# Three chunks of modulation weights move from the second attention into the FFN before it, with a ring of four piece buffers and three accumulators

## What is computed

```python
c_act = jax.nn.silu(c)
for layer in range(DEPTH_2):
    mod = (c_act @ ada_w[layer] + ada_b[layer]).reshape(B, 3, 3, D_MODEL)
    h = modulate(x, norm_g[layer, 0], mod[:, 0, 0], mod[:, 0, 1])
    x = x + 0.5 * mod[:, 0, 2][:, None, :] * swiglu(h, ffn_w13[layer, 0], ffn_w2[layer, 0])
    h = modulate(x, norm_g[layer, 1], mod[:, 1, 0], mod[:, 1, 1])
    y = swa_mixer(...) if layer % N_MIXERS == 0 else fox_mixer(...)
    x = x + mod[:, 1, 2][:, None, :] * y
    h = modulate(x, norm_g[layer, 2], mod[:, 2, 0], mod[:, 2, 1])
    x = x + 0.5 * mod[:, 2, 2][:, None, :] * swiglu(h, ffn_w13[layer, 1], ffn_w2[layer, 1])
```

## Time and profile before

| | |
|---|---|
| median of 3 runs | 1521.77 us (1520.66 to 1526.52) |
| profiled execution | 1525.41 us |
| its span, first to last instruction | 1523.60 us |
| mean granted TensorE clock | 0.969 |
| PE busy | 1424.1 us (93%) |
| DVE busy | 1083.2 us (71%) |
| ACT busy | 732.8 us (48%) |
| POOL busy | 140.3 us (9%) |
| moved by DMA | 333.89 MB, mean 219 GB/s |

### The profile page before, as it was taken

The page is one execution under the profiler, slowest core; times in us unless marked ns, Lnnn a source line. Parts: engine busy times, 40 slices in busy tenths (PEclk is TensorE's granted clock), DMA queues, the critical chain, the costliest instruction groups (busy, mean ns, idle before and its releaser), DMA issues.

```text
span 1523.6 us, 18395 instructions
## 1 busy us (share of the span) xinstructions
PE 1424.1 (93%) x7241; PEld 1170.0 (77%) x7241; DVE 1083.2 (71%) x1523; ACT 732.8 (48%) x1036; POOL 140.3 (9%) x198
## 2 busy tenths in 40 slices
PE   2799898999999999988899999999999899999998
PEld 1588887999978877765688777787877766688886
DVE  5867885988977777767578777777777445566544
ACT  3454355444564433766463334644437566554432
POOL 1100100110101111000001111011120100000000
PEclk9899999999999999995999999999999989999999
DMA  9776664877859888461478887598883631376552
GB/s 355 237 226 204 229 213 143 270 254 246 307 180 311 291 280 290 140 221 28 141 244 300 295 284 256 179 309 296 282 282 115 197 110 56 111 243 199 177 184 81
DMA packets 189289, 333.89 MB, mean 219 GB/s; under 512 B 8834, under 2 KB 132462, under 8 KB 188180
## 3 DMA queue, kind: packets, MB, share of 16 engines
q1 hardware_dynamic: 161392, 236.02, 45.8%
q0 software_dynamic: 27232, 96.47, 19.3%
q10 hardware_dynamic: 580, 0.23, 0.1%
HBM read 331.53 MB, written 1.15 MB: 218 GB/s over the span
## 4 chain that ended last, share of the span: by engine, by line
PE 66%; DVE 15%; DMA 8%; ACT 6%; issue 4%; SPq 0%; ACTq 0%; POOL 0%; DVEq 0%; POOLq 0%
DMA ada<-in_ada_w 8%; PE bank L1449 8%; PE bank L1451 8%; PE bank L1450 8%; PE bank L1412 7%; PE bank L1414 6%; PE bank L1413 6%; DVE lo L942 5%; DVE ada_sum L901 4%; PE bank L1344 3%; PE bank L1345 3%; PE bank L1346 3%; ACT hi L514 2%; PE bank L1577 2%; PE bank L1650 2%
## 5 line engine op out<-in xcount | busy, mean ns | idle before, releaser
L942 DVE TENSOR_TENSOR lo<-raw,hi 128x2048 fp32r<-128x2048 f32 x215 | 490.9, 2286 | 67.3 <-ACT hi L514 66.8
L514 ACT ACTIVATE hi<-raw 128x2048 fp32r<-128x2048 f32 x215 | 405.6, 1909 | 34.6 <-DMA raw<-in_w_out 20.8
L1449 PE MATMUL bank<-hi,h_hi 128*128 128x512 f32 x704 | 277.9, 395 | 2.4 <-DVE lo L942 1.6
L901 DVE SCALAR_TENSOR_TENSOR ada_sum<-ada,c_act,ada_sum 128x512 f32<-128x512 f32 x308 | 231.1, 750 | 67.0 <-DMA ada<-in_ada_w 59.2
L1451 PE MATMUL bank<-hi,h_lo 128*128 128x512 f32 x704 | 274.5, 390 | 0.0
L1450 PE MATMUL bank<-lo,h_hi 128*128 128x512 f32 x704 | 274.1, 389 | 0.0
L470 POOL DMA_DIRECT2D ada<-in_ada_w x176 | 125.6, 714 | 1126.9 <-DVE ada_sum L901 1087.6
L1412 PE MATMUL bank<-hi,o_hi 128*128 128x512 f32 x504 | 206.1, 409 | 12.2 <-DVE lo L942 11.1
L1414 PE MATMUL bank<-hi,o_lo 128*128 128x512 f32 x504 | 198.3, 393 | 0.0
L1413 PE MATMUL bank<-lo,o_hi 128*128 128x512 f32 x504 | 197.8, 392 | 0.0
L625 ACT ACTIVATE KT<-bank 128x256 f32<-128x256 f32 x88 | 33.8, 384 | 315.9 <-PE bank L1451 315.8
(11 more groups left out here) (208 smaller groups left out, 1838.2 us busy)
## 6 DMA issues: line engine op xcount, KB each, us to landing
ada<-in_ada_w POOLq DMA_DIRECT2D x176, 512.0 KB, 5.3
raw<-in_ffn_w SPq DMA_DIRECT2D x176, 512.0 KB, 5.1
raw<-in_ffn_w SPq DMA_DIRECT2D x44, 1024.0 KB, 6.1
raw<-in_w_up SPq DMA_DIRECT2D x22, 1024.0 KB, 5.5
raw<-in_w_in SPq DMA_DIRECT2D x16, 1024.0 KB, 8.3
raw<-in_fox_w_in SPq DMA_DIRECT2D x12, 1024.0 KB, 5.1
raw<-in_w_down SPq DMA_DIRECT2D x11, 1024.0 KB, 6.2
raw<-in_swa_w_in SPq DMA_DIRECT2D x6, 1024.0 KB, 5.1
```

Source lines behind the costliest of these rows:

```text
L514: nc.scalar.activation(hi[:, n % NS, :], raw[:, n % NS, :], ACT.Copy).then_inc(hi_ready, 1)
L901: nc.vector.scalar_tensor_tensor(acc, in0=src, scalar=c_act[:, col:col + 1], in1=acc, op0=ALU.mult, op1=ALU.add).then_inc(ada_step, 1)
L942: nc.vector.tensor_tensor(lo[:, n % NS, :], raw[:, n % NS, :], hi[:, n % NS, :].bitcast(F32), ALU.subtract).then_inc(lo_ready, 1)
L1449: mm(bank[:, :], xk_hi, wh[:, i, :], start=k == 0, stop=False, skip_group_check=True)
```

## The change

The FFN before the second attention takes in twelve chunks in place of nine, and the attention none in place of three. Since twelve chunks are 48 pieces over 26 units, from unit 2 on (before: 36 over 27, from unit 3 on), the tables of that stage are drawn up anew: two pieces on most of the units 2 to 26, one on the units 8, 14, 21 and 27. From the second stage on the pieces go round four buffers: two of `ada` and two in `V`, which POOL may fill once the attention before has read its last values (and the first attention's pooling branch is done); in turn ACT waits with an attention's first value copy until all pieces of the stages before are used (L669). The accumulators `ada_sum` are three. In the first attention three turned sums, their column sums and a gate stand one unit later. At the entrance of the conv stage ACT and DVE take the second half of the rows before unit 3 and not behind it. The constants that were one tile (`kon`) are three tiles with two loads; two unused parts of them are no longer loaded. (`ident` becomes `ident[:, :]` in PE's calls, `c % 2` becomes `c % 3` where accumulators are read, `n % 2` becomes `slot`; these lines are not shown.)

```diff
-CHUNKS_IN = [6, 6, 9, 3, 9, 9, 0, 2]
+CHUNKS_IN = [6, 6, 12, 0, 9, 9, 0, 2]
+RING_FROM = PIECES * CHUNKS_IN[0]
...
     if kind0 in ("conv", "ffn"):
-        at = [3 + (p0 * 27 // (4 * n0) if n0 > 4 else p0) for p0 in range(4 * n0)]
...
+        from0, over = (2, 26) if n0 > 10 else (3, 27)
         turns, at_sums = [], []
-        for u1 in (at[4 * c0 + 3] + 2 for c0 in range(n0)):
+        for c0 in range(n0):
+            for p0 in range(4 * c0, 4 * c0 + 4):
+                u0 = from0 + (p0 * over // (4 * n0) if n0 > 4 else p0)
+                if c0 > 2:
+                    u0 = max(u0, at_sums[c0 - 3])
+                PIECES_AT[w0 + u0] = PIECES_AT.get(w0 + u0, 0) + 1
+            u1 = u0 + 2
...
-        SUMS_AT.update({w0 + u: 1 for u in (7, 9, 13, 16, 18, 21)})
-        COLS_AT.update({w0 + u: 1 for u in (8, 10, 14, 17, 19, 22)})
-        GATES_AT[w0 + 15], GATES_AT[w0 + 20] = (s0, 0), (s0, 1)
-    elif kind0 == "swa":
-        PIECES_AT[w0 + 4] = 2
-PIECES_STEP = {"moba": (), "swa": range(8, 16), "fox": ()}
-SUMS_STEP = {"moba": (), "swa": (1,), "fox": ()}
-COLS_STEP = {"moba": (), "swa": (2,), "fox": ()}
-SUMS_LAST = {"swa": 2, "fox": 0}
+        SUMS_AT.update({w0 + u: 1 for u in (7, 9, 13, 17, 19, 22)})
+        COLS_AT.update({w0 + u: 1 for u in (8, 10, 14, 18, 20, 23)})
+        GATES_AT[w0 + 15], GATES_AT[w0 + 21] = (s0, 0), (s0, 1)
...
-        ada_sum = sb("ada_sum", [P, 2, 512])
+        ada_sum = sb("ada_sum", [P, 3, 512])
...
+        def piece_slot(n):
+            if n < RING_FROM:
+                return n % 2, n // 2 + 1
+            q = n % 4
+            return q, (n - RING_FROM) // 4 + 1 + (RING_FROM // 2 if q < 2 else 0)
+
+        def piece_of(n):
+            q, _ = piece_slot(n)
+            return ada[:, q, :, :] if q < 2 else V[:, q - 2, :].rearrange("p (a b) -> p a b", a=2)
...
-                    if n > 1:
-                        pool.wait_ge(ada_step, 2 * (n - 1))
+                    slot, _ = piece_slot(n)
+                    if n < 2:
+                        pool.wait_ge(pro_step, KD)
                     else:
-                        pool.wait_ge(pro_step, KD)
-                    pool.dma_start(ada[:, n % 2, :, :], ...).then_inc(ada_full[n % 2], 16)
+                        earlier = n - 2 if n < RING_FROM + 4 else n - 4
+                        pool.wait_ge(ada_step, 2 * (earlier + 1))
+                    if slot >= 2:
+                        before = sum(n >= PIECES * sum(CHUNKS_IN[:s + 1]) for s in ATTENTIONS)
+                        pool.wait_ge(pv_done, (8, 24, 40)[before - 1])
+                        if before == 1:
+                            pool.wait_ge(pool_ready, 4)
+                    pool.dma_start(piece_of(n), ...).then_inc(ada_full[slot], 16)
...
                 if KINDS[b] == "conv":
                     normed(b, 1)
+                    modulated(b, 1)
                     split_to(W0[b] + 3)
...
+                if s and v == 0:
+                    act.wait_ge(ada_step, 2 * PIECES * sum(CHUNKS_IN[:s]))
...
                     if c >= PRO_CHUNKS + 3:
                         dve.wait_ge(ada_used, c - 2 - PRO_CHUNKS)
...
                     root(b, 1)
                     split_to(W0[b] + 2)
+                    split_h(b, 1)
+                    split_to(W0[b] + 3)
                 else:
                     split_to(W0[b] + 2)
                     root(b, 1)
-                split_to(W0[b] + 3)
-                split_h(b, 1)
+                    split_to(W0[b] + 3)
+                    split_h(b, 1)
...
-                columns(int(t in COLS_STEP[kind]))
-                pieces(int(t in PIECES_STEP[kind]))
...
-                    pieces(2)
...
-                    columns(2)
...
-                sums(int(t in SUMS_STEP[KINDS[s]]))
...
-                last = SUMS_LAST[kind]
-                if last:
-                    pe.wait_ge(olo_done, (HEAD0[s] + HEADS[kind]) // 2)
-                    sums(1)
                 step_out(s, 3, 0)
-                sums(last // 2)
```

More of the change, by code:

```diff
@@ L58 @@
 PIECES = 4
-CHUNKS_IN = [6, 6, 9, 3, 9, 9, 0, 2]
+CHUNKS_IN = [6, 6, 12, 0, 9, 9, 0, 2]
+ATTENTIONS = [s for s, k in enumerate(KINDS) if k in HEADS]
+RING_FROM = PIECES * CHUNKS_IN[0]
 FFN_ORDER = ([(0, 0), (0, 1), (1, 0), (1, 1), (0, 2)]
@@ L73 @@
     if kind0 in ("conv", "ffn"):
-        at = [3 + (p0 * 27 // (4 * n0) if n0 > 4 else p0) for p0 in range(4 * n0)]
-        for u0 in at:
-            PIECES_AT[w0 + u0] = PIECES_AT.get(w0 + u0, 0) + 1
+        from0, over = (2, 26) if n0 > 10 else (3, 27)
         turns, at_sums = [], []
-        for u1 in (at[4 * c0 + 3] + 2 for c0 in range(n0)):
+        for c0 in range(n0):
[5 more added lines that the diff above has]
+            u1 = u0 + 2
             if len(at_sums) > 1 and len(turns) < 2 and u1 >= at_sums[-1] + 2:
@@ L113 @@
 ROWS_LOADED = 23 * 16
-SMALL_LOADED = 8 * 16
+SMALL_LOADED = 9 * 16
 def chunk_of(c):
@@ L162, in build @@
         cols = sb("cols", [P, 512])
-        kon = sb("kon", [P, K_END])
+        ident = sb("ident", [P, P])
+        mask = sb("mask", [P, 2 * P])
+        inverses = sb("inverses", [P, 64])
         ones = sb("ones", [P, P])
@@ L221, in build @@
         pro_full = [sem(f"pro_full{n}") for n in range(8)]
-        ada_full = [sem(f"ada_full{n}") for n in range(2)]
+        ada_full = [sem(f"ada_full{n}") for n in range(4)]
         rows_full, small_full, x_full = sem("rows_full"), sem("small_full"), sem("x_full")
@@ L438, in _ @@
         def _(pool):
-            pool.dma_start(kon[:, P:K_END], consts[:, P:K_END]).then_inc(small_full, 16)
+            pool.dma_start(mask[:, :], consts[:, K_MASK:K_MASK + 2 * P]).then_inc(small_full, 16)
+            pool.dma_start(inverses[:, :], consts[:, K_INV:K_END]).then_inc(small_full, 16)
             pool.dma_start(tables, buckets).then_inc(small_full, 16)
@@ L570, in boundary @@
                     normed(b, 1)
-                modulated(b, 1)
+                    modulated(b, 1)
             def gate_copy(s, half):
@@ L890, in ada_op @@
             def ada_op(c, k, src):
-                acc = ada_sum[:, c % 2, :]
+                acc = ada_sum[:, c % 3, :]
                 col = (0 if chunk_of(c)[0] < 2 else 8) + k
@@ L895, in ada_op @@
                 if k == 0:
-                    if c >= PRO_CHUNKS + 2:
-                        dve.wait_ge(ada_used, c - 1 - PRO_CHUNKS)
+                    if c >= PRO_CHUNKS + 3:
+                        dve.wait_ge(ada_used, c - 2 - PRO_CHUNKS)
                     nc.vector.tensor_scalar(acc, src, c_act[:, col:col + 1], None, ALU.mult).then_inc(ada_step, 1)
@@ L908, in pieces @@
                     c, q = PRO_CHUNKS + n // PIECES, n % PIECES
-                    dve.wait_ge(ada_full[n % 2], 16 * (n // 2 + 1))
+                    slot, count_to = piece_slot(n)
+                    dve.wait_ge(ada_full[slot], 16 * count_to)
                     for i in range(2):
-                        ada_op(c, 2 * q + i, ada[:, n % 2, i, :])
+                        ada_op(c, 2 * q + i, piece_of(n)[:, i, :])
                     next_piece += 1
@@ L1136, in pool_branch @@
                 mean = sq[:, 2, 0:16]
-                step(nc.vector.tensor_tensor(mean, have[:, 0:16], kon[:, K_INV + 16 * g:K_INV + 16 * (g + 1)], ALU.mult))
+                step(nc.vector.tensor_tensor(mean, have[:, 0:16], inverses[:, 16 * g:16 * (g + 1)], ALU.mult))
                 dst = std[:, g // 2, T * (g % 2):T * (g % 2 + 1)]
@@ L1745, in _ @@
             for t in range(4):
-                ins = nc.tensor.transpose(G[0][:, P * t:P * (t + 1)], rows[:, t, :], ident)
+                ins = nc.tensor.transpose(G[0][:, P * t:P * (t + 1)], rows[:, t, :], ident[:, :])
             ins.then_inc(rows_turned, 1)
@@ L1764, in _ @@
                         first = D * part + 512 * h + P * i
-                        ins = nc.tensor.transpose((M, S)[part][:, P * i:P * (i + 1)], pro_sum[:, first:first + P], ident)
+                        ins = nc.tensor.transpose((M, S)[part][:, P * i:P * (i + 1)], pro_sum[:, first:first + P], ident[:, :])
                     ins.then_inc(pro_turned, 1)
```

24 lines of the change are left out of this document (10 added, 14 removed).

## The result

| | before | changed |
|---|---|---|
| median | 1524.14 us (4 runs, 1520.66 to 1531.16) | 1503.74 us (4 runs, 1500.69 to 1506.10) |
| profiled execution | 1525.41 us | 1500.69 us |
| its span | 1523.60 us | 1498.90 us |

The ratio is 0.986, with a 95% interval of 0.982 to 0.990: the change is 1.4% faster, some 20 us. In two later sets of runs the same kernel had 0.984 (0.981 to 0.987) and 0.985 (0.981 to 0.988). The forecast was faster by 7.2 us, with 1505 us as the low end of the range.

The account below looks back on a forecast made before the run. FFN stages were taken as close to PE's own time, with idle or slow time in the attention and at stage boundaries. Terms -4.8 - 4.6 + 1.8 + 2.4 + 2.0 - 4.0 = -7.2 us gave a 1514.6 us median; range 1505 to 1523.

Parts of the forecast that it names:

- +2.0: Twelve-chunk FFN, steady part: late piece transfers add 2.0 us; ends -2.2 (all stalls by late pieces go) and +8.3.
- the forecast's own case: Whole kernel: faster by 3 to 12 us; chance 0.60, a little over half of it beyond 7.6 us.
- the clock in the attention: Rival, second attention: PE's full clock returns earlier or the fall does not happen, whole 1504 to 1511 us; chance 0.15.
- Conv entrance: Conv stage's entrance: `h_lo` comes 3.4 us earlier and the clock gives 1.4 (ends 0 and -2.4), together -4.8 us.
- First attention: Three turned sums, column sums and a gate move one unit: 0, with 0.6 us to either side.
- Second attention: Without 12 pieces on DVE, three turned sums on PE and their column sums, the stage gains 4.6 us.
- +1.8: Twelve-chunk FFN: three more turned sums come in where PE is full, costing 1.8 us.
- +2.4: Twelve-chunk FFN's entrance: two pieces now stand ahead of the reciprocal `root`, costing 2.4 us; ends 0 and 2.9.
- the transfers saturate: Rival, twelve-chunk FFN: transfers can't exceed 284 GB/s, each step takes 2.9 us more, whole 1538 us; chance 0.08.
- DVE becomes the bound: Rival, twelve-chunk FFN: a step takes 19.5 us, +8.2 in place of +2.0, whole 1520.8 us; chance 0.15.
- Later FFNs: Two later nine-chunk FFNs: the deeper ring removes PE's waits behind late DVE multiplications, -4.0 us; ends 0 and -5.3.
- a ring that does nothing: Rival: the two buffers in `V` come late, later FFNs win nothing, -3.2 us, whole 1518.6 us; chance 0.02.

Follow-up runs that it names:

- the kernel with nine and three chunks: The changed kernel with nine chunks in the FFN and three in the second attention again, ring and three accumulators kept, two buffers in the attention: 1509.05 us, ratio 0.987.

## Why the prediction was right in its direction and too small

The step that failed is the term "+2.0" for late transfers in the FFN with twelve chunks: it gave the ring and the third accumulator no gain in that stage, and they gave 5.0 us. The measured time lies beyond the forecast's own case (-3 to -12 us), and no rival stood for that side but the clock in the attention, which did not come about. One of the prediction's own signs of being wrong, that FFN below 205 us, did: it lasted 202.6.

**Conv entrance** (-4.8): right. 2.22 us of idle time (forecast 2.3); -4.5 without the clock, -6.0 with it. The -1.4 for the clock lay between two cases that both occur.

**First attention** (0, 0.6 to either side): the step failed in its argument "the work is the same and PE was busy there". Between the moved instructions stand pieces whose transfer takes about 5 us, so DVE's order decides whether it waits for them. +1.4 us here, 1 to 3 by the later runs.

**Second attention** (-4.6): right. -5.1 against the kernel with nine and three chunks, -6.1 in the pair of profiles, all three at a granted clock of 0.81 or 0.82. "The clock in the attention comes back early" (0.15) did not happen as a consequence: PE ran at half clock in 672 to 713 us, about as long as before, and where the clock did come back (0.86 to 0.88 in other profiles) it did so with the pieces in the attention too.

```profile
672.00:713.00 41.00, 36.56 (x105) 21.22 (x106) 28.72 (x94) 27.26 (x71) 0.00 (x0) 0.50 0.06 19
```

**FFN with twelve chunks** (+1.8, +2.4, +2.0): the step that failed. The first two were roughly right (the entrance +1.5; three more chunks and the entrance together +3.6). The third, "+2.0, nearer to the lower end", priced a risk, late transfers, and gave the ring nothing. Nine chunks with ring and accumulators take 199.0 us, 5.0 less than before. My lower end was -2.2, the measured term -5. The +2.0 itself has no run behind it: what twelve chunks add to nine, 3.6 us, is less than the 4.2 of the first two terms. The third accumulator stood in no term at all, and without it the stage takes 221.3 us. A stretch of 56 us in the steady part of the changed kernel, against the earlier trace rows:

```profile
529.90:586.00 56.10, 56.10 (x267) 46.57 (x266) 53.91 (x66) 23.72 (x22) 12.80 (x18) 1.00 1.00 350
```

PE is never idle, at 350 GB/s and with DVE busy for 96%. The rivals "the transfers saturate" (it decided below 312 GB/s) and "DVE becomes the bound" both fall, the second by a narrow margin: 2.2 us are left in 56. The queues' full-share rates that I took from the earlier trace rows, 329 and 339 GB/s, were too low. Over 22 us, 452 to 474, they moved 368:

```profile
452.00:474.00 22.00, 22.00 (x106) 18.24 (x106) 16.80 (x20) 8.71 (x10) 2.95 (x5) 1.00 1.03 368
```

The Trainium skill ("DMA: Bandwidth & Descriptors", Specifications) gives about 358 GB/s as the HBM limit of one core, which it gets as half of what a stack gives to two. Only one core runs here: the 350 over 56 us stay below that figure, and the 368 over 22 us lie above it, so over that time it is not a limit here. My sum without the transfers' term would have been 2 us nearer, and no more.

**Later FFNs** (-4.0, ends 0 and -5.3): right in kind, outside its own bounds in size: -6.0 and -2.9. The end of -5.3 took two kinds of PE's waits. All of PE's idle time was 6.0 and 4.1 us in these stages and is 2.1 and 2.1 now, which is 5.9; the other 3 us went out of what counts as busy. One such place, before:

```profile
930.53 0.39 PE L1450 MATMUL bank<-lo,h_hi 128*128 128x512 f32 x1
930.76 0.39 PE L1451 MATMUL bank<-hi,h_lo 128*128 128x512 f32 x1
933.33 0.66 PE L1380 MATMUL bank<-kon,ada_sum 128*128 128x128 f32 x4 [2.18 <-DVE KT L1029]
933.74 0.47 PE L1449 MATMUL bank<-hi,h_hi 128*128 128x512 f32 x1
934.05 0.39 PE L1450 MATMUL bank<-lo,h_hi 128*128 128x512 f32 x1
```

In a full stream these products start every 0.23 us though a row says 0.39; the last one before a wait shows its whole 0.39, and the first behind it takes 0.31 to the next. The idle row is 2.18, and the two traces part by 2.4 us there. At the waits of 0.97 and 0.71 us in front of turning a hidden block they part by 1.3 and 1.0 us.

In sum: -7.2 forecast, about -20 in medians and -24.7 in the profiled pair. The 17.5 us between forecast and pair are 7.6 in the twelve-chunk FFN, 4.9 in the later FFNs, 2.7 in conv and second attention and 5.0 in the last two stages (the clock), less 2.6 in start-up and first attention. The rival of a ring that does nothing did not occur.

## What to carry to other kernels

A wait of an engine that is not the bound (here 17 us a stage of DVE for late pieces) is read as harmless as long as its own busy share is 71%; but where its order is fixed and the bounding engine waits for single instructions in it, deeper buffering gives time back even when the engine's load rises. Price such a change by all idle time of the bounding engine in the stage, not by the one or two waits that name the cause, and take the stage's own best case (an FFN without pieces in its way) as the far end. And spread filler work evenly: four pieces behind one unit gave PE a wait of 3 us, and half clock behind it, that two and two did not. Where an engine waits for transfers anyway, leave it filler work to do there (the column sums of the first attention). Before a stage's difference is laid to an edit, compare its granted clock in both profiles.

## What the runs showed of the hardware that I had not expected

- An idle row of PE understates a wait in a dense stream: 2.18 us in the row, 2.4 between the traces; 0.97 and 1.3; 0.71 and 1.0.
- A single wait of 2.99 us in a dense stream was followed by PE at half clock (0.50 in 455 to 457 us) in the kernel with four pieces behind unit 4.
- 350 GB/s were held over 56 us with PE never waiting, and 368 over 22 us, on one core.
- TensorE's clock in the attention stages varies within one kernel: the last attention had 0.93, 0.97 and 0.98 and 154.6, 150.2 and 148.6 us with the same work on all engines. The second attention had 0.81 and 114.1 us or 0.88 and 110.7 with the same instructions. A pair of profiles can differ by 5 us for that alone, while the changed kernel's FFN stages repeat within 0.1 us.
